# Second attention in steps of two head pairs, with the Fourier and output units dealt out in halves

## What is computed

```
xn = rms_norm(x) * (1 + sc_x) + sh_x
f_in, f_gate, q, k, v, na_gate = split(xn @ w_in)          # 512 columns each
f_out  = (real(fft2(f_in)) * scale @ w_four) * silu(f_gate)
# 8 heads of 64; a query attends to a window of 16 grid columns in all 8 grid rows, and to 256 context keys
s      = concat(q @ k_window + bias, q @ k_ctx) * scale
na_out = (softmax(s) @ concat(v_window, v_ctx)) * silu(na_gate)
x_new  = x + g_x * (concat(f_out, na_out) @ w_out)
```

## Time and profile before

| | |
|---|---|
| median of 3 runs | 930.6 us (930.52 to 930.89) |
| span of the profiled execution, first to last instruction | 927.6 us |
| what lies around the span (median less span) | 3.0 us |
| second attention, from its first scores to the last products | 784.95 to 896.71 us, 111.76 us |
| TensorE busy | 903.8 us, 97% of the span |
| VectorE, ScalarE, GpSimd busy | 39%, 23%, 18% |

### The profile page before, as it was taken

One profiled execution on the slowest core, in us unless ns is written; L12 is line 12 of the kernel. 1 busy time (PEld: TensorE's weight loads), 2 busy tenths in 40 slices (PEclk: granted clock), 3 DMA queues, 4 the chain that ended last, 5 costly groups with the idle time before them and its releaser, 6 DMA issues.

```text
span 927.6 us, 13379 instructions
## 1 busy us (share of the span) xinstructions
PE 903.8 (97%) x5548; PEld 509.0 (55%) x5548; DVE 364.6 (39%) x802; ACT 215.0 (23%) x468; POOL 165.1 (18%) x159
## 2 busy tenths in 40 slices
PE   7999999999999989999999999999999999999998
PEld 3588874445565443343343333344688888755553
DVE  1765542357664463210210210047545543444431
ACT  2211213345555200010110110123202111632310
POOL 3212220000003044130230200042202211440000
PEclk9999999999999999999999999999999999999999
DMA  9935559024010978999999999961472012600002
GB/s 330 306 109 182 182 194 398 21 91 182 1 46 0 313 187 308 401 407 428 425 420 427 423 426 427 400 205 41 120 196 91 24 45 58 216 1 1 1 12 79
DMA packets 71453, 188.47 MB, mean 203 GB/s; under 512 B 31184, under 2 KB 31840, under 8 KB 65120
## 3 DMA queue, kind: packets, MB, share of 16 engines
q1 hardware_dynamic: 62416, 162.41, 47.4%
q0 software_dynamic: 5488, 18.37, 5.4%
q10 hardware_dynamic: 3488, 6.82, 1.9%
HBM read 168.70 MB, written 18.89 MB: 202 GB/s over the span
## 4 chain that ended last, share of the span: by engine, by line
PE 88%; DVE 4%; DMA 2%; POOL 2%; ACT 2%; issue 2%; SPq 0%; DVEq 0%; POOLq 0%; ACTq 0%
PE psum L920 20%; PE psum L1114 18%; PE psum L1135 8%; PE psum L1021 6%; PE psum L842 6%; PE psum L1265 5%; PE psum L946 5%; PE psum L969 5%; PE psum L983 3%; PE psum L1000 2%; PE psum L1333 2%; PE psum L1048 1%; PE psum L1227 1%; PE psum L1365 1%; POOL qk_st L2505 1%
## 5 line engine op out<-in xcount | busy, mean ns | idle before, releaser
L1114 PE MATMUL psum<-ring,buf_a 128*32 128x512 f32 x1536 | 169.0, 592 | 3.5 <-issue 3.5
L1114 PEld LDWEIGHTS psum<-ring,buf_a 128*32 128x32 f32 x1536 | 60.8, 110 | 107.4 <-issue 107.1
L1135 PE MATMUL psum<-ring,buf_c 128*32 128x512 f32 x768 | 86.1, 593 | 0.4 <-issue 0.4
L2578 POOL DMA_INDIRECT buf_b<-xq_d,o_sb x48 | 51.7, 1077 | 159.6 <-DVE buf_a L2193 129.6
L2216 DVE TENSOR_TENSOR buf_c<-buf_c,psum 128x512 f32<-128x512 f32 x12 | 13.1, 1088 | 156.4 <-PE psum L1114 156.4
L2505 POOL TENSOR_TENSOR qk_st<-qk_st,half 128x8 f32<-128x8 f32 x26 | 43.6, 1678 | 158.3 <-DVE qk_st L2275 72.9
L920 PE MATMUL psum<-ring,buf_a 128*128 128x256 f32 x320 | 70.9, 380 | 0.0
L920 PE MATMUL psum<-ring,buf_b 128*128 128x256 f32 x288 | 64.8, 380 | 0.0
L920 PEld LDWEIGHTS psum<-ring,buf_a 128*128 128x128 f32 x320 | 60.1, 190 | 8.2 <-issue 0.4
L1021 PE MATMUL psum<-ring,buf_b 128*128 128x512 f32 x128 | 59.8, 594 | 0.0
L1841 DVE TENSOR_TENSOR s_buf<-s_buf,psum 128x512 f32<-128x512 f32 x52 | 35.3, 686 | 61.2 <-PE psum L920 57.8
(11 more groups left out here) (302 smaller groups left out, 1159.2 us busy)
## 6 DMA issues: line engine op xcount, KB each, us to landing
ring<-in_moe_w_gate SPq DMA_DIRECT2D x16, 2048.0 KB, 12.2
ring<-in_moe_w_up SPq DMA_DIRECT2D x16, 2048.0 KB, 15.0
ring<-in_moe_w_down SPq DMA_DIRECT2D x16, 2048.0 KB, 16.0
ring<-in_w_in SPq DMA_DIRECT2D x7, 2048.0 KB, 15.2
ring<-in_w_ada SPq DMA_DIRECT2D x6, 2048.0 KB, 9.5
ring<-in_da_w_in SPq DMA_DIRECT2D x5, 2048.0 KB, 21.3
y_d<-ring POOLq DMA_DIRECT2D x1, 5632.0 KB, 21.9
y_d<-buf_b ACTq DMA_DIRECT2D x11, 512.0 KB, 11.4
```

What stands on the lines that cost most here:

```text
L1114: last = mm(buf("mm", n)[rows, :], x_part[:, j, k, :], slot(moe_load(q, m, r))[:, k, :], start=(k == 0), stop=(k == KD - 1))
L1135: last = mm(buf("sc", n)[rows, m, :], hidT[:, s % 3, f * P + SUB * j:f * P + SUB * (j + 1)], slot(moe_load(q, 2, r), FC)[:, f, m * CH:(m + ...
L2578: pool.indirect_dma_start(out=xg[:, s % 2, j * 256:(j + 1) * 256], out_offset=None, in_=xn_quarters, in_offset=bass.IndirectOffsetOnAxis(a ...
```

## The change

The steps become nine, each with two pairs. Step i has scores 2i and 2i + 1, then pv 2i - 2 and 2i - 1, in even steps from 2 on a gate for tile i / 2 - 1 (its diag, on VectorE, stands behind the scores of the same step), then half a unit, pT 2i, the other half of the unit, and pT 2i + 1. Fourier units 4 and 5 and the out_f units are cut into two halves of eight instructions with one "sc" buffer; the smaller Fourier units 0 to 3 stay whole and take the places of halves, two to a step. out_last is cut 2, 2 and 4 products, and the piece of four now stands in front of the last two pv; nothing but the last gate stands behind them. VectorE's reads of a halved unit follow its second half. Since two pT now precede their two pv, ScalarE's copies go to pT and pd in turn.

```diff
@@ -210,38 +210,40 @@
-FOURIER_AT = [0, 1, 3, 4, 6, 8]
-OUT_AT = [10, 12, 14]
-OUT_LAST = [(0, 3), (3, 5), (5, 8)]
+MIXER_STEPS = PAIRS // 2 + 1
+OUT_LAST = [(0, 2), (2, 4), (4, 8)]
+BEFORE_PT = [[], [("fourier", 2)], [("fourier", 4)], [("fourier", 5)],
+             [("out_f", 0)], [("out_f", 1)], [("out_f", 2)], [("out_last", 0)], []]
+AMID_PT = [[("fourier", 1)], [("fourier", 3)], [("fourier_rest", 4)], [("fourier_rest", 5)],
+           [("out_f_rest", 0)], [("out_f_rest", 1)], [("out_f_rest", 2)], [("out_last", 1)], []]
...
-def mixer_steps(s):
+def mixer_steps(i):
+    first, second = 2 * i, 2 * i + 1
+    c = i // 2 - 1 if i >= 2 and i % 2 == 0 else None
     todo = []
-    if s < PAIRS:
-        todo.append(("scores", s))
-    if s in FOURIER_AT:
-        todo.append(("fourier", FOURIER_AT.index(s)))
-    if s in OUT_AT:
-        todo.append(("out_f", OUT_AT.index(s)))
-    if s >= PAIRS:
-        todo.append(("out_last", s - PAIRS))
-    if 2 <= s < PAIRS + 2:
-        todo.append(("pv", s - 2))
-    for name, at in (("diag", 4), ("gate", 5)):
-        c, late = divmod(s - at, 4)
-        if 0 <= c < TT and late == 0:
-            todo.append((name, c))
-    if 1 <= s <= PAIRS:
-        todo.append(("pT", s - 1))
-    if s == PAIRS + 1:
+    if i == 0:
+        todo += [("scores", first), ("fourier", 0), ("scores", second)]
+    elif first < PAIRS:
+        todo += [("scores", first), ("scores", second)]
+    else:
         todo.append(("out_last", 2))
+    if c is not None:
+        todo.append(("diag", c))
+    if i >= 1:
+        todo += [("pv", first - 2), ("pv", second - 2)]
+    if c is not None:
+        todo.append(("gate", c))
+    todo += BEFORE_PT[i]
+    if first < PAIRS:
+        todo.append(("pT", first))
+    todo += AMID_PT[i]
+    if second < PAIRS:
+        todo.append(("pT", second))
     return todo
-
-
-MIXER_STEPS = PAIRS + 2
...
+    probs_T = [pT, pd]
...
-        def out_products(n, t, first):
-
-            claim(pe, "sc", n)
-            for a in range(2):
+        def out_products(n, t, first, halves=(0, 1)):
+
+            if halves[0] == 0:
+                claim(pe, "sc", n)
+            for a in halves:
...
-            fill(last, "sc", n)
+            if halves[-1] == 1:
+                fill(last, "sc", n)
...
+                elif name in ("fourier", "fourier_rest"):
+                    n, b = turn["sc", "fourier", m], int(name == "fourier_rest")
+                    w = chunk2("w_four", 4)
+                    if b == 0:
+                        claim(pe, "sc", n)
+                        drained(pe, "sc", turn["sc", "fourier", 2])
+                        drained(pe, "sc", turn["sc", "fourier", 3])
+                    f = 2 * (m - 4) + b
+                    for k in range(4):
+                        last = mm(buf("sc", n)[:, b, :], w[:, k, f * P:(f + 1) * P], yT[:, k, :],
+                                  start=(k == 0), stop=(k == 3))
+                    if b == 1:
+                        fill(last, "sc", n)
...
-                    out_products(turn["sc", "out_f", m], m, 0)
+                    out_products(turn["sc", "out_f", m], m, 0, (0,) if name == "out_f" else (1,))
...
-                                      pT[:, hh, b * P:(b + 1) * P], start=(b == 0), stop=(b == 3))
+                                      probs_T[m % 2][:, hh, b * P:(b + 1) * P],
+                                      start=(b == 0), stop=(b == 3))
...
-                        drain(S.copy(pT[:, hh, :], buf("tp", n)), "tp", n)
+                        drain(S.copy(probs_T[m % 2][:, hh, :], buf("tp", n)), "tp", n)
...
-                elif name == "fourier" and m >= 4:
+                elif name == "fourier_rest":
...
-                elif name == "out_f":
+                elif name == "out_f_rest":
```

## The result

The changed kernel took 932.13 us (931.57 to 937.51, 7 runs), the kernel before 930.52 (929.35 to 930.89, 7 runs). The ratio is 1.0034, 95% interval 1.0018 to 1.005. The medians lie 1.6 us apart, which is a factor of 1.0017; the means, into which the two high executions of 934.0 and 937.51 go, lie 2.9 us apart. A second comparison, with 12 and 23 runs, gave 1.0023 (1.0005 to 1.0042). One of the twelve, of 946.06 us, is a slow execution and is left out of the ratio. The forecast was 932.7 and a span of 929.7.

The account below looks back on a forecast made before the run. TensorE, 88% of the chain, was taken as the bound; 5.0 us saved in shape changes against new waits gave +2.1 us, span 927.6 to 929.7, plus 3.0 around it 932.7 us, against 930.6. Range 930.2 to 934.4, own range 931.8 to 933.8.

Parts of the forecast that it names:

- What goes: From scores 0 to the last products, 57 changes of weight shape on TensorE become 27, saving 5.0 us.
- scores behind scores keep a slot of 1.07: Sign that the forecast is wrong: merged scores on TensorE not getting shorter; it expected two scores in 1.95 us.
- (a): In steps 1, 3, 5 and 7 the unit waits for ScalarE's exponential to free its buffer, 0.65 us each.
- (b): In steps 2, 4 and 6 the gate waits for its diagonals on VectorE, 2.10 us, covering the unit's buffer wait.
- (c): Scores 5 wait for ScalarE and VectorE to read Fourier unit 3's buffer; 0.7 us in the sum.
- (d): The last products wait for VectorE's mixT behind the last gate, 1.58 us, with no out_last work to cover it.
- Gate 0: First gate: diagonals on VectorE take 1.59 us beside GpSimd's scaling; the skill's rule could add 0.9, taken as 0.
- The sum: Whole stage: +2.1 us by walking the steps; check: waits 12.2 against 4.8 before, +7.4, less 5.0 saved, +2.4.
- Rival 1: Faster: each of 30 changes of shape costs more than slots show, 0.30 giving 929.0 us; chance 0.12.
- rival 3: Slower still: scores behind scores and pv behind pv drain too, losing 2.6 us of the saving, 935.3; chance 0.07.
- Rival 2: Nearly the same: 0.20 per change of shape (6.0 us saved), first diagonals at 1.23: +1.0, 931.6; chance 0.18.
- Rival 4: Slower: clock falls to 1.2 GHz in a wait, one half unit adding 3.4 us, 936.1; chance 0.03.

Follow-up runs that it names:

- kinds apart: Scores, pv, scores, pv in steps 1 to 7 instead of scores, scores, pv, pv, against the changed kernel: 935.4 us, ratio 1.0068 to the kernel before.

## Why the prediction was right

The time, 932.13, lies 0.6 below the forecast of 932.7 and inside both of its ranges; the sign was right, and 1.0034 is clear of 1. Step by step:

- **What goes.** Forecast 5.0 us from 30 changes of shape. In slots, the stage without waits fell from 107.0 (111.76 - 4.8) to 102.5 (113.68 - 11.1): 4.4, or 0.15 a change. The term was somewhat too large: the first of two scores takes 0.97, but the second takes 1.07 and not 0.97 before the following pv. Two scores take 2.04, where the forecast had 1.95 and two unmerged ones take 2.14, so its sign "scores behind scores keep a slot of 1.07" came true for the second of the two and not for the first. About 0.1 in each of up to seven steps is 0.7 at most. It cost nothing here, since a wait followed every time; with diag early nothing waits behind it in steps 4 and 6.
- **(a) the unit's buffer.** Forecast 0.65 in four steps, measured 0.54 in slots; the start at 4.48 into the step was right, TensorE came 0.1 later.
- **(b) the gate.** Start 5.79 and 5.84 into the step, forecast 5.84; wait 1.95 and 2.01 instead of 2.10, for the same 0.1. Moving diag away gave back 5.9 us, so the price is shown by experiment, and the late diag on the old order cost 5.9 by itself. The forecast named diag's place in the gate's own step, and that is the cause; that it stands behind two pairs instead of one is not.
- **(c) scores 5.** 0.65 instead of 0.7.
- **(d) the last gate.** 1.59 against 1.58; undoing it gave 1.62.
- **Gate 0.** The first diagonals took 1.42 us, not 1.59:

```profile
812.12 1.42 DVE L2470 TENSOR_TENSOR o_sb<-ident,rden 128x1024 f32<-128x1024 f32 x1
```

In the eleven profiles of this case the first diagonals, always beside GpSimd's scaling, took 1.23 to 2.14 us (1.59 before, 1.42 here, 1.25 with kinds apart, 2.14 in the old order with late diag), and the later ones, without it, 1.22 or 1.23. The rule of the Trainium skill (SBUF — State Buffer, Who interferes with whom) that I had given no weight, that one of the two waits for the other's whole instruction, allows for the 2.05 and 2.14 (up to 1.3 more than 1.23); by the row of before alone it could not have been foreseen.
- **The sum.** +2.1 forecast for the stage, +1.92 measured: the saving was 0.6 too large, and the waits, 12.2 in the forecast's check and 11.1 measured, were too long. In part this is one error, since TensorE waits less where it comes later to a wait. (The terms of that check add up to 12.1, not 12.2, which leads to +2.3.) The span was forecast at 929.7 and was 929.8 in the profiled execution.
- **What lies around the span.** This term was wrong in size, if little: 3.0 us, the median less the span of one profiled execution. Executions whose own span is recorded have 1.7 to 1.8 (931.57 with 929.8). The profiled execution of before was simply a short one: in the second comparison that kernel's median span is 928.6, not 927.6. The profiled execution of the changed kernel was the shortest of its seven too, and the execution at the median has a span of 930.4. So that the time lies only 0.6 off is in part luck: a base one microsecond too short and a surrounding 1.2 too long took each other away.
- **Rivals.** Rival 1 (more than 0.25 a change) and rival 3 (merged kinds drain as well) are out, by the slots and by the kinds set apart. Rival 2 had the direction of one of its two terms, the first diagonals (1.42, between its 1.23 and the 1.59 kept), and was wrong in the other: the 30 changes saved 4.4 us, not 6.0. Rival 4, the clock, is real: I gave it 0.03, and the mean clock was under 1.000 in 8 of 19 executions of the changed kernel. The one of these that was profiled has its fall behind a gate, at 1.7 us instead of 3.4, because the clock was back before the half unit was through. It does not carry the median: executions with a clock of 1.000 lie at 929.96 to 932.45. It explains the upper end of the runs in part only: 937.51 has a mean clock of 0.998, like 931.95, so most of what it lies higher has another cause, which stays open. What I read as evidence against it, waits up to 0.96 at full clock, said nothing of waits twice as long.

## What to carry to other kernels

Count changes of weight shape on TensorE, and price one from the trace, by comparing the same group in front of an equal and an unequal neighbour; here it was 0.15 to 0.20 us by the rows, and 30 changes fewer saved 4.4 us. Then walk every other engine's queue through the new order. When two steps become one, work that used to stand a step ahead of its reader (here the diagonals) can slip into the reader's own step, and that alone cost 5.9 us, in the old order as in the new: it must stay a step ahead. And the last piece of filling work must stay behind the last dependency. With both put right, the same change gained 0.7% instead of losing 0.2% to 0.3%.

## What the runs showed of the hardware

- A wait of TensorE of 1.84 to 3.00 us in this stage was followed in seven cases of eleven by a stretch at half the granted clock, right behind the wait, at about 1.7 us each; with three waits of 2.1 us it came three times in one execution. The highest times of the changed kernel (937.51, and 946.06 in the second comparison) are above those of the kernel before (930.89 and 936.27), but the mean clock accounts for them only in part.
- Of two scores groups (64x128) one behind the other the first took 0.97 and the second 1.07 before a pv. The second saves nothing against a group by itself (1.07), though no change of shape stands in front of it. Why is not shown.
- The same VectorE instruction on two SBUF operands took 1.23 to 2.14 us beside GpSimd's scaling, and 1.22 or 1.23 without it.
